# Padding the slots of the split weight tiles by 64 bytes in a two-block fp32 network

## The chip, the cores and the metric

One core of a Trainium2 chip runs the whole program. The metric is device time in microseconds, the median of three runs. The kernel before takes 2099.29 us (2099.01 to 2099.45).

## The reference

Two blocks of a sequence model act on x (512 positions, 1024 features, fp32). Cut to what matters:

```python
# first block
proj = rms_norm(x) @ w_in                        # 1024 -> 7184
merged = g_ml*(mlstm(...) @ w_br_ml) + g_na*(neighbourhood(...) @ w_br_na) + g_xa*(cross(...) @ w_br_xa)
x = x + merged @ w_out
x = x + (gelu(conv3(a)) * u) @ w_down            # a, u = split(rms_norm(x) @ w_up), 1024 -> 2 x 2816 -> 1024
# second block, layer 0
x = x + (b * conv3(c * h)) @ w_out               # b, c, h = split(rms_norm(x) @ w_in)
x = x + (silu(conv3(a)) * g) @ w_down            # the same feed-forward shape
# second block, layer 1
x = x + gated_forgetting_attention(x) @ w_out    # 16 heads of 64
x = x + (silu(conv3(a)) * g) @ w_down
out = rms_norm(x)
```

Nearly all of the arithmetic is products of a 512 x 1024 (or 512 x 2816) activation with an fp32 weight matrix.

## The kernel before

Activations are kept transposed: features on the 128 partitions, the 512 positions along the free axis, so a 1024-feature activation is `KB` = 8 blocks of 128 x 512. A weight matrix is cut into **units** of 128 output features. A unit is one 128 x 1024 tile, whose 8 blocks of 128 x 128 are the stationary operands; the activation block is the moving operand.

To be accurate enough each fp32 value is held as two values of the type fp32r, a high and a low part. Activations have XH and XL (for the feed-forward FH and FL, for others AH/AL, YH/YL, GH/GL). Weights have WH and WL. Each block of a unit takes three matmuls (`unit`, lines 1652 to 1654, and the same triple in other functions): high weights on high activations, high weights on low activations, low weights on high activations.

```python
mm(dst[:, 0:width], WH[:, s, w], a, ...)   # w = slice(k * P, (k + 1) * P)
mm(dst[:, 0:width], WH[:, s, w], b, ...)
mm(dst[:, 0:width], WL[:, s, w], a, ...)
```

A unit passes through four steps, each on its own engine, over `NSLOT` = 4 slots of the tiles RAW, WH and WL:

- SP issues the load of the raw unit into `RAW[:, s, :]`.
- ACT rounds it to WH (`hi`, line 655, one instruction of 1024 columns).
- POOL writes RAW minus WH to WL (`lo`, line 519, four instructions of 256 columns).
- PE multiplies.

The slot is the unit's number modulo four. The loops are unrolled by multiples of four, so each slot's address is a constant of the instruction.

A few places use the slots differently. `forget_unit` (lines 1949 and 1950) takes 48 columns of each block. `lo_gate` and `lo_forget` see a slot as blocks of 32 or 128 columns with a rearranged view. `value_blocks` (lines 1965 to 1967) exchanges the roles: there blocks of XH and XL are stationary, and 512 columns of WH or WL are moving. The attention parts are plain fp32, not fp32r, and don't use these tiles. In `bout_ends` copies of the last blocks stand in tiles of their own.

Where tiles lie is written by hand. `fixed` places them one after another, and X begins at a multiple of 512 bytes (`line`). In each partition X, XH, XL, RAW, WH and WL then take 16 KiB each, the small tiles follow, and after them, at the next multiple of 512, the `zone` that the later tiles share (function `at`, offsets in KiB). A block of 128 weights is 512 bytes of a partition, so every stationary block in WH and WL begins at a multiple of 512 bytes, and so does every moving block of 512 columns.

Of the kernel before, what the change touches and what calls it, by code (L numbers as in the profile page):

```python
# [13 lines left out]
F32R = mybir.dt.float32r  # L14
ALU = mybir.AluOpType
ACT = mybir.ActivationFunctionType
AX = mybir.AxisListType

P = 128
# [8 lines left out]
NSLOT = 4  # L28
LO_PARTS = 4
UW = KB * P  # L30
EPS = 1e-6
NEG = -1e30
ML_H, XA_H, FA_PAIRS, NA_PAIRS = 4, 4, 8, 4
# [155 lines left out]
def two_blocks(nc, A, out):  # L189
# [4 lines left out]
    def fixed(name, shape, dt=F32):  # L194
        t = nc.alloc_sbuf_tensor_at(name, shape, dt, offset=top[0])
        n = 4
        for d in shape[1:]:
            n *= d
        top[0] += (n + 31) // 32 * 32
        return t  # L200
# [13 lines left out]
    XH = fixed("XH", [P, KB, S], F32R)  # L214
    XL = fixed("XL", [P, KB, S], F32R)
    RAW = fixed("RAW", [P, NSLOT, UW])
    WH = fixed("WH", [P, NSLOT, UW], F32R)
    WL = fixed("WL", [P, NSLOT, UW], F32R)
    R = fixed("R", [P, S])
    RM = fixed("RM", [P, M])  # L220
    SS = fixed("SS", [P, S])
# [17 lines left out]
    PAR = fixed("PAR", [P, NCOL])  # L239
    UT = fixed("UT", [P, TB, 64])  # L240
    zone = (top[0] + line - 1) // line * line
    assert zone + 91 * 1024 <= nc.sbuf_usable_end, (zone, nc.sbuf_usable_end)

    def at(name, kib, shape, dt=F32):
        n = 4
        for d in shape[1:]:
            n *= d
        assert kib * 1024 + n <= 91 * 1024
        return nc.alloc_sbuf_tensor_at(name, shape, dt, offset=zone + int(kib * 1024))

    Y = at("Y", 0, [P, 12, S])
    MEMT = at("MEMT", 0, [P, KB, M])
    SX = at("SX", 24, [P, 2, S])
    PT = at("PT", 28, [P, 2, S])
    PB = at("PB", 32, [P, 2, S])
# [59 lines left out]
    hi_ready, lo_ready, unit_done = sem("hi_ready"), sem("lo_ready"), sem("unit_done")  # L315
# [67 lines left out]
    def width(u):  # L383

        j = u - U["merge"]
        return UW // 2 if 0 <= j < len(MRG) and MRG[j][0] == "br" else UW

# [4 lines left out]
    def f_name(p, s):  # L392

        return ("k", "q")[s] if p < FA_LAST else ("q", "k")[s]
# [5 lines left out]
    def f_bank(p, use):  # L400

        return LB[(O["fa"] + FA_L * p + FA_USE[p][use]) % 2]
# [13 lines left out]
    def _(sp):  # L416
        def load(u0, j, i, per, src, width):

            s = (u0 + j) % NSLOT
            if u0 + j >= NSLOT:  # L420
                sp.wait_ge(lo_ready, i * per + (u0 + j - NSLOT + 1))
            sp.dma_start(RAW[:, s, 0:width], src).then_inc(raw_full[s], 16)

        def stream(name, w, iters, per):

            with sp.Fori(0, iters) as i:
                for j in range(per):
                    load(U[name], j, i, per, w[bass.ds(i * per + j, 1), :, :].rearrange("o p n -> p (o n)"), UW)

# [12 lines left out]
        for u in range(NATT):  # L442
            load(0, u, 0, 0, A["w_att"][u, :, :], UW)
            if u < 2:
# [67 lines left out]
    def _(pool):  # L512
        def lo(u0, j, i, per):
# [3 lines left out]
            for c in range(parts):  # L517
                w = slice(c * UW // LO_PARTS, (c + 1) * UW // LO_PARTS)
                last = nc.gpsimd.tensor_tensor(WL[:, s, w], RAW[:, s, w], WH[:, s, w].bitcast(F32), ALU.subtract)  # L519
                if u0 == 0 and j < 2 and c < parts - 1:  # L520
# [3 lines left out]
        def lo_forget():  # L524

            s = U["f"] % NSLOT
            pool.wait_ge(hi_ready, U["f"] + 1)
            raw, w = (t[:, s, :].rearrange("p (k c) -> p k c", c=P) for t in (RAW, WH))
            nc.gpsimd.tensor_tensor(w[:, :, 32:48], raw[:, :, 0:16], w[:, :, 0:16].bitcast(F32), ALU.subtract)\
                .then_inc(lo_ready, 1)  # L530

        def lo_gate(u):

            s = u % NSLOT
            pool.wait_ge(hi_ready, u + 1)
            raw, w = (t[:, s, :].rearrange("p (n c) -> p n c", c=32) for t in (RAW, WH))
            pool.wait_ge(r_ready, 1)
            nc.gpsimd.memset(SS[:], 0.0)
            pool.drain()
            nc.gpsimd.tensor_tensor(w[:, :, 16:32], raw[:, :, 0:16], w[:, :, 0:16].bitcast(F32), ALU.subtract)\  # L540
                .then_inc(lo_ready, 1)
# [5 lines left out]

        for t, v in ((TA[:, 0:P], 1.0), (TA[:, P:2 * P], 0.0), (IDN[:], 0.0), (LO[:], 1.0), (UP[:], 1.0), (EPSC[:], EPS), (ZERO[:], 0.0)):
            nc.gpsimd.memset(t, v).then_inc(consts, 1)
        pool.wait_ge(consts, 7)  # L550
        nc.gpsimd.tensor_copy(ONER[:], TA[:, 0:P])
        nc.gpsimd.memset(EPSC[:, 1:2], EPS * EPS)
        nc.gpsimd.memset(TA[0:64, P:P + 64], 1.0)
# [11 lines left out]
        for u in range(NATT):  # L565
# [4 lines left out]
            if u in BIAS_UNITS:  # L570

                p, v = BIAS_UNITS[u]
# [25 lines left out]
        los("up1", 11, 4)  # L598
        los("down1", 2, 12)
        lo_forget()  # L600

        def causal(dst, src):
# [20 lines left out]
        def lo_parted(n):  # L623
# [3 lines left out]
            for w in [slice(c * 2 * P, min((c + 1) * 2 * P, KEND)) for c in range(LO_PARTS)]:  # L627
                nc.gpsimd.tensor_tensor(WL[:, s, w], RAW[:, s, w], WH[:, s, w].bitcast(F32), ALU.subtract)
            nc.gpsimd.tensor_tensor(WEL[:, n, :], RAW[:, s, KEND:UW], WEH[:, n, :].bitcast(F32), ALU.subtract)\
# [14 lines left out]
    def _(act):  # L644
        A_ = nc.scalar.activation

        def hi(u0, j, i, per):

            if not isinstance(i, int) or u0 + j + i * per < NUNITS:
# [4 lines left out]
                w = slice(0, width(u0 + j))  # L654
                A_(WH[:, s, w], RAW[:, s, w], ACT.Copy).then_inc(hi_ready, 1)  # L655

# [53 lines left out]
        for t, (un, st) in enumerate(SLOTS):  # L710
# [21 lines left out]
            if m < 4 * ML_H:  # L732

                h, s = m // 4, m % 4
# [8 lines left out]
                for d in range(2):  # L743
                    w = slice(P * s, S) if d == 0 else slice(0, P * (s + 1))
                    A_(SXM[m % 2][:, d, w], UE[:, h, d, w], ACT.Relu, bias=UT[:, s, 32 * d + h:32 * d + h + 1])
                act.drain()
                for d in range(2):
                    w = slice(P * s, S) if d == 0 else slice(0, P * (s + 1))
# [40 lines left out]
            if un and un[0] in HALF:  # L789
                k = sum(1 for x in UNITS[:u] if x[0] in HALF)  # L790
# [3 lines left out]
                elif un[0] == "mg":  # L794
                    q = un[1]
                    c = (2 - q % 3) * KB + q // 3
# [4 lines left out]
            if t and EXTRA[t - 1][:1] and EXTRA[t - 1][0][:2] == ("tr", "nav"):  # L801

                p = EXTRA[t - 1][0][2]
# [20 lines left out]
        for j, (kind, n, b) in enumerate(MRG):  # L824
            hi(U["merge"], j + AHEAD, 0, 0)
            if kind == "mg":
                done += 1
                c = (2 - b) * KB + n
# [96 lines left out]
        def hi_parted(n):  # L925
# [4 lines left out]
            if n == 0:  # L930
                act.wait_ge(fc_out, 16)
            A_(WH[:, s, 0:KEND], RAW[:, s, 0:KEND], ACT.Copy)
            A_(WEH[:, n, :], RAW[:, s, KEND:UW], ACT.Copy).then_inc(hi_ready, 1)

        def hi_behind(n):

            s = (U["bout"] + n) % NSLOT
            act.wait_ge(raw_full[s], 16 * ((U["bout"] + n) // NSLOT + 1))
            act.wait_ge(bout_read, n - NSLOT + 1)
            A_(WH[:, s, :], RAW[:, s, :], ACT.Copy).then_inc(hi_ready, 1)  # L940

        def squared(p, s):

# [103 lines left out]
        turned(FA_LAST, 0)  # L1047
        exps(FA_LAST, 1)
        hi_behind(4)
        turned(FA_LAST, 1)  # L1050
        exps(FA_LAST, 2)
        hi_behind(5)
        turned(FA_LAST, 2)
        hi_behind(6)
        hi_behind(7)
        residual("bout", 2, 4, 4, "fg2", unrolled=lambda j: None, have=KB - AHEAD)
# [5 lines left out]
    def _(dve):  # L1062
# [457 lines left out]
        def head_sums(p, s):  # L1520

            dve.wait_ge(q_rs, 2 * p + s + 1)
            n = f_name(p, s)
            v.scalar_tensor_tensor(out=SS[:], in0=f_bank(p, n + "s")[:], scalar=64 * EPS, in1=TD[:],
                                   op0=ALU.add, op1=ALU.mult).then_inc(lin_free, 1)
# [108 lines left out]
    def _(pe):  # L1634
        mm = nc.tensor.matmul

        def unit(u0, j, i, per, kc, xh, xl, k0, dst, start=True, stop=True, width=S, ready=None, halfway=None):
# [4 lines left out]
            for k in range(kc):  # L1642
# [10 lines left out]
                mm(dst[:, 0:width], WH[:, s, w], b, start=False, stop=False)  # L1653
                last = mm(dst[:, 0:width], WL[:, s, w], a, start=False, stop=stop and k == kc - 1)  # L1654
            last.then_inc(unit_done, 1)
# [118 lines left out]
        for t, (un, st) in enumerate(SLOTS):  # L1774
# [37 lines left out]
            if un:  # L1812
# [5 lines left out]
                if t == 0:  # L1818
                    for n, (tt, part, ks) in enumerate(START_ORDER):
# [3 lines left out]
                        for k in ks:  # L1823
# [8 lines left out]
                            else:  # L1832
                                if tt < 2 and k < KB - 2:
                                    pe.wait_ge(first_lo[tt], k // 2 + 1)
                                else:
                                    pe.wait_ge(lo_ready, tt + 1)
                                last = mm(bb[:], WL[:, tt, w], XH[:, k, :], start=False, stop=ends)
                        if n == START_LAST[tt]:
# [5 lines left out]
                elif t < 5:  # L1844
# [7 lines left out]
                    for k in range(KB):  # L1852
                        last = mm(b[:], WL[:, t % NSLOT, k * P:(k + 1) * P], XH[:, k, :], start=False, stop=k == KB - 1)
                    last.then_inc(unit_done, 1)
# [20 lines left out]
        def linear(name, iters, per, xh, xl, ready, norm_of=None, halfway=None, two=0):  # L1875


            def part(j, k0, k1):
# [6 lines left out]
                for k in range(k0, k1):  # L1885
# [4 lines left out]
                    mm(bank_[:], WH[:, s, w], b, start=False, stop=False)  # L1890
                    last = mm(bank_[:], WL[:, s, w], a, start=False, stop=k == KB - 1)  # L1891
                if k1 == KB:
# [326 lines left out]
```

## Time and profile before

| what | value |
|---|---|
| median of 3 runs | 2099.29 us |
| profiled execution, first to last instruction (its own time) | 2098.1 us |
| PE busy | 2090.3 us, 9860 matmul records |
| PEld (weight loads) busy | 1709.4 us, 9860 loads |
| POOL busy | 1164.5 us |
| DVE busy | 972.7 us |
| ACT busy | 884.3 us |
| granted TensorE clock, mean | 1.000 |
| DMA | 203.70 MB, 97 GB/s |

The busy time of PE counts records that overlap: a matmul's record begins when its columns begin to stream and ends when the last result has left, so the pace is read from the distance between the starts of two records, not from the duration of one. PEld is the loading of stationary operands, which runs beside PE. Clock 1.000 means that the granted clock was the higher of its two levels, 2.4 GHz, throughout.

### The profile page before, as it was taken

How to read it: one execution, taken by the hardware profiler on the slowest of the kernel's cores; microseconds unless marked ns; L12 is line 12 of the kernel's file. 1: busy time of each engine (PE TensorE's matmuls, PEld its weight loads, DVE VectorE, ACT ScalarE, POOL GpSimd, SP SyncE). 2: the span in 40 equal slices, each digit the busy share in tenths (PEclk: the TensorE clock that was granted, in tenths of full speed). 3: DMA queues.
4: the chain of work that ended last, by engine and by line, in shares of the span. 5: the costliest groups of instructions: out<-in, count | busy, mean ns of one | idle time of the engine just before them, and what ended most of it. 6: DMA issues, size and time to landing. Idle time of an engine off the chain costs nothing.

```text
span 2098.1 us, 29633 instructions
## 1 busy us (share of the span) xinstructions
PE 2090.3 (100%) x9860; PEld 1709.4 (81%) x9860; DVE 972.7 (46%) x1682; ACT 884.3 (42%) x1355; POOL 1164.5 (56%) x1554
## 2 busy tenths in 40 slices
PE   9999999999999999999999999999999999999999
PEld 7788888888888888888888888888777778888887
DVE  6567564334455551234445544213377755545300
ACT  5544556223434343332244344224466655434321
POOL 8553346556555556555455656565544536556653
PEclk9999999999999999999999999999999999999999
DMA  6333222323332333323233333333322213333332
GB/s 234 119 99 114 63 64 70 106 78 123 92 100 93 96 94 102 95 91 100 91 101 100 96 94 89 108 94 101 111 81 81 81 61 101 100 100 90 103 92 76
DMA packets 62667, 203.70 MB, mean 97 GB/s; under 512 B 7056, under 2 KB 8720, under 8 KB 62576
## 3 DMA queue, kind: packets, MB, share of 16 engines
q1 hardware_dynamic: 60624, 201.54, 30.9%
q10 hardware_dynamic: 1952, 0.99, 0.2%
q8 instruction: 52, 0.85, 0.2%
q14 instruction: 39, 0.32, 0.0%
HBM read 199.42 MB, written 2.26 MB: 96 GB/s over the span
## 4 chain that ended last, share of the span: by engine, by line
PE 98%; DVE 1%; DMA 0%; DVEq 0%; ACT 0%; issue 0%; ACTq 0%; SPq 0%
PE bank L1652 28%; PE bank L1654 28%; PE bank L1653 28%; PE bank L1992 1%; PE bank L2018 1%; PE bank L1761 1%; PE bank L2004 1%; PE bank L1706 1%; PE bank L1965 1%; PE bank L1967 1%; PE bank L1966 1%; PE bank L1891 1%; PE bank L1889 1%; PE bank L1890 1%; PE bank L2049 1%; PE bank L1802 1%
## 5 line engine op out<-in xcount | busy, mean ns | idle before, releaser
L519 POOL TENSOR_TENSOR WL<-RAW,WH 128x256 fp32r<-128x256 f32 x1424 | 1105.8, 809 | 865.7 <-ACT WH L655 858.8
L1652 PE MATMUL bank<-XH,WH 128*128 128x512 f32 x1688 | 661.2, 392 | 0.3 <-DVE FG L1571 0.3
L1654 PE MATMUL bank<-XH,WL 128*128 128x512 f32 x1688 | 657.2, 389 | 0.0
L1653 PE MATMUL bank<-XL,WH 128*128 128x512 f32 x1688 | 656.9, 389 | 0.0
L655 ACT ACTIVATE WH<-RAW 128x1024 fp32r<-128x1024 f32 (+1 forms) x366 | 372.9, 1023 | 236.1 <-PE bank L1654 208.4
L1652 PEld LDWEIGHTS bank<-XH,WH 128*128 128x128 f32 x1688 | 316.9, 188 | 68.4 <-issue 2.8
L1654 PEld LDWEIGHTS bank<-XH,WL 128*128 128x128 f32 x1688 | 316.9, 188 | 66.7
L1653 PEld LDWEIGHTS bank<-XL,WH 128*128 128x128 f32 x1688 | 317.0, 188 | 64.5
L1652 PE MATMUL bank<-FH,WH 128*128 128x512 f32 x528 | 205.4, 389 | 0.0
L1653 PE MATMUL bank<-FL,WH 128*128 128x512 f32 x528 | 205.4, 389 | 0.0
L1654 PE MATMUL bank<-FH,WL 128*128 128x512 f32 x528 | 205.4, 389 | 0.0
L1399 DVE TENSOR_TENSOR X<-X,bank 128x512 f32 (+1 forms) x48 | 32.9, 685 | 292.4 <-PE bank L1654 283.9
L882 ACT ACTIVATE TD<-TC 128x512 f32<-128x512 f32 x66 | 41.7, 632 | 278.0 <-DVE TC L1143 188.0
L1143 DVE SCALAR_TENSOR_TENSOR TC<-TA,PAR,TC 128x511 f32<-128x511 f32 (+1 forms) x134 | 108.9, 813 | 22.4 <-issue 21.8
L1653 PEld LDWEIGHTS bank<-FL,WH 128*128 128x128 f32 x528 | 99.1, 188 | 20.7
L1654 PEld LDWEIGHTS bank<-FH,WL 128*128 128x128 f32 x528 | 99.1, 188 | 20.7
L1652 PEld LDWEIGHTS bank<-FH,WH 128*128 128x128 f32 x528 | 99.1, 188 | 20.4
L1429 DVE TENSOR_TENSOR TA<-bank,R 128x512 f32<-128x512 f32 x66 | 45.6, 691 | 124.1 <-PE bank L1654 116.1
L1434 DVE TENSOR_TENSOR TE<-bank,R 128x512 f32<-128x512 f32 x66 | 45.6, 691 | 110.0 <-PE bank L1654 110.0
L885 ACT ACTIVATE FH<-TA 128x512 f32 x66 | 41.8, 633 | 126.3 <-DVE TA L1438 126.3
L1440 DVE TENSOR_TENSOR FL<-TA,FH 128x512 f32 x66 | 60.1, 911 | 61.7 <-ACT FH L885 61.7
L849 ACT ACTIVATE XH<-X,PAR (+1 forms) x40 | 29.0, 724 | 134.9 <-DVE X L1399 134.9
(336 smaller groups left out, 2618.5 us busy)
## 6 DMA issues: line engine op xcount, KB each, us to landing
RAW<-in_w_up SPq DMA_DIRECT2D x132, 512.0 KB, 3.5
RAW<-in_w_att SPq DMA_DIRECT2D x50, 512.0 KB, 3.6
RAW<-in_w_down SPq DMA_DIRECT2D x48, 448.0 KB, 3.2
RAW<-in_w_down SPq DMA_DIRECT2D x24, 512.0 KB, 3.5
RAW<-in_w_ain SPq DMA_DIRECT2D x24, 512.0 KB, 3.4
RAW<-in_w_fa SPq DMA_DIRECT2D x24, 512.0 KB, 3.6
RAW<-in_w_mrg SPq DMA_DIRECT2D x15, 512.0 KB, 3.9
RAW<-in_w_mrg SPq DMA_DIRECT2D x24, 256.0 KB, 2.7
```

The costliest lines, as they stand in the source:

```text
L519: last = nc.gpsimd.tensor_tensor(WL[:, s, w], RAW[:, s, w], WH[:, s, w].bitcast(F32), ALU.subtract)
L655: A_(WH[:, s, w], RAW[:, s, w], ACT.Copy).then_inc(hi_ready, 1)
L882: A_(TD[:], TC[:], fn).then_inc(glu_ready, 1)
L885: A_(blk(FH, i * 2 + n), TA[:], ACT.Copy).then_inc(ffh_ready, 1)
L1143: last = v.scalar_tensor_tensor(out=TC[:, -d:S], in0=c[:, 0:S + d], scalar=w[k], in1=TC[:, -d:S], op0=ALU.mult, op1=ALU.add)
L1399: v.tensor_tensor(blk(X, nn), blk(X, nn), b[:], ALU.add).then_inc(lin_free, 1)
L1429: v.tensor_tensor(TA[:], LB[0 if (O[name] % 2) == 0 else 1][:], R[:], ALU.mult)\
L1434: v.tensor_tensor(TE[:], LB[1 if (O[name] % 2) == 0 else 0][:], R[:], ALU.mult)\
L1440: v.tensor_tensor(blk(FL, nn), TA[:], blk(FH, nn).bitcast(F32), ALU.subtract).then_inc(ffl_ready, 1)
L1652: mm(dst[:, 0:width], WH[:, s, w], a, start=start and k == 0, stop=False)
L1653: mm(dst[:, 0:width], WH[:, s, w], b, start=False, stop=False)
L1654: last = mm(dst[:, 0:width], WL[:, s, w], a, start=False, stop=stop and k == kc - 1)
```

## The change

A slot of WH and of WL becomes 1040 values long instead of 1024; the last 16 values (64 bytes) are never written or read. RAW keeps 1024. The places that took a whole slot of WH now name its first 1024 columns.

Worked out from the code: WH still begins at a multiple of 512 bytes, and its slots s = 0 to 3 now begin at the remainders 0, 64, 128 and 192 of 512. WH is 256 bytes longer, so WL begins at the remainder 256, and its slots at 256, 320, 384 and 448. WL is 256 bytes longer too, so all that follows it moves by 512 bytes, and so does the zone: their remainders stay as they were. Only the bound on the zone's size falls, from 91 to 90 KiB. The order and the number of instructions on all engines, and of the DMAs, are the same.

```diff
+WPAD = 16
...
-    WH = fixed("WH", [P, NSLOT, UW], F32R)
-    WL = fixed("WL", [P, NSLOT, UW], F32R)
+    WH = fixed("WH", [P, NSLOT, UW + WPAD], F32R)
+    WL = fixed("WL", [P, NSLOT, UW + WPAD], F32R)
...
-    assert zone + 91 * 1024 <= nc.sbuf_usable_end, (zone, nc.sbuf_usable_end)
+    assert zone + 90 * 1024 <= nc.sbuf_usable_end, (zone, nc.sbuf_usable_end)
...
-        assert kib * 1024 + n <= 91 * 1024
+        assert kib * 1024 + n <= 90 * 1024
...
@@ lo_forget
-            raw, w = (t[:, s, :].rearrange("p (k c) -> p k c", c=P) for t in (RAW, WH))
+            raw, w = (t[:, s, 0:UW].rearrange("p (k c) -> p k c", c=P) for t in (RAW, WH))
...
@@ lo_gate
-            raw, w = (t[:, s, :].rearrange("p (n c) -> p n c", c=32) for t in (RAW, WH))
+            raw, w = (t[:, s, 0:UW].rearrange("p (n c) -> p n c", c=32) for t in (RAW, WH))
...
@@ the rounding of a unit of the attention's output product, on ACT
-            A_(WH[:, s, :], RAW[:, s, :], ACT.Copy).then_inc(hi_ready, 1)
+            A_(WH[:, s, 0:UW], RAW[:, s, :], ACT.Copy).then_inc(hi_ready, 1)
```

## Rows read from the trace of the kernel before

**Rows 1.** The page: span, then busy time and instructions by engine.

```profile
span 2098.1 us, 29633 instructions
...
PE 2090.3 (100%) x9860; PEld 1709.4 (81%) x9860; DVE 972.7 (46%) x1682; ACT 884.3 (42%) x1355; POOL 1164.5 (56%) x1554
```

**Rows 2.** The page, chain that ended last: shares of the span by line.

```profile
PE bank L1652 28%; PE bank L1654 28%; PE bank L1653 28%; PE bank L1992 1%; PE bank L2018 1%; PE bank L1761 1%; PE bank L2004 1%; PE bank L1706 1%; PE bank L1965 1%; PE bank L1967 1%; PE bank L1966 1%; PE bank L1891 1%; PE bank L1889 1%; PE bank L1890 1%; PE bank L2049 1%; PE bank L1802 1%
```

**Rows 3.** Whole span, L1652 alone: PE busy (x), PEld busy (x), PEclk, DMA share, GB/s.

```profile
0.00:2098.10 2098.10, 1012.11 (x2600) 488.29 (x2600) 1.00 0.31 97
```

**Rows 4.** Timeline of PE from 599.8 us: start us, us, line, operands, shape.

```profile
599.81 0.39 PE L1652 MATMUL bank<-XH,WH 128*128 128x512 f32 x1
600.04 0.39 PE L1653 MATMUL bank<-XL,WH 128*128 128x512 f32 x1
...
603.89 0.39 PE L1652 MATMUL bank<-XH,WH 128*128 128x512 f32 x1
```

**Rows 5.** Timeline of PE's weight loads (PEld) at 600 us.

```profile
599.81 0.19 PEld L1653 LDWEIGHTS bank<-XL,WH 128*128 128x128 f32 x1
```

**Rows 6.** Timeline of PE, forget unit: stationary operands of 48 columns from WH.

```profile
1440.38 0.40 PE L1949 MATMUL bank<-XH,WH 128*48 128x512 f32 x1
...
1444.15 0.39 PE L1965 MATMUL bank<-WH,XH 128*128 128x512 f32 x1
```

**Rows 7.** Weight loads of three lines: duration ns min/median/max, first and last start.

```profile
L1652 PEld LDWEIGHTS bank<-XH,WH x1688: 186/188/192, 38.4 to 1974.1; 128*128 128x128 f32 x188
...
L1950 PEld LDWEIGHTS bank<-XL,WH x8: 122/122/124, 1440.4 to 1443.7; 128*48 128x48 f32 x8
...
L2018 PEld LDWEIGHTS bank<-FP,FY x320: 132/137/138, 1524.8 to 1709.2; 128*64 128x64 f32 x160
```

**Rows 8.** Timeline of PE, memory keys: moving operands of 256 columns.

```profile
85.28 0.28 PE L1653 MATMUL bank<-ML,WH 128*128 128x256 f32 x1
...
86.00 0.28 PE L1653 MATMUL bank<-ML,WH 128*128 128x256 f32 x1
```

**Rows 9.** Timeline of PE, mLSTM heads in plain fp32: products, scores.

```profile
223.72 1.05 PE L1761 MATMUL bank<-V,PT 128*128 128x129 f32 x8
224.61 0.39 PE L1761 MATMUL bank<-V,PB 128*128 128x129 f32 x2
...
230.32 1.02 PE L1802 MATMUL bank<-Q,K 128*128 128x512 f32 x2
231.18 0.38 PE L1761 MATMUL bank<-V,PT 128*128 128x129 f32 x2
...
330.14 0.61 PE L1761 MATMUL bank<-V,PT 128*128 128x129 f32 x4
330.58 0.61 PE L1761 MATMUL bank<-V,PB 128*128 128x129 f32 x4
```

**Rows 10.** Timeline of PE, after a wait at 508 us.

```profile
507.99 0.50 PE L1652 MATMUL bank<-GH,WH 128*128 128x512 f32 x1 [0.22 <-DVE X L1399]
508.33 0.40 PE L1653 MATMUL bank<-GL,WH 128*128 128x512 f32 x1
...
510.66 0.39 PE L1654 MATMUL bank<-GH,WL 128*128 128x512 f32 x1
```

**Rows 11.** First 50 us, all engines' busy time (x); then PEclk, DMA share, GB/s.

```profile
2.00:50.00 48.00, 47.06 (x220) 37.02 (x219) 30.22 (x59) 28.96 (x50) 40.65 (x72) 1.00 0.69 249
```

**Rows 12.** Timeline of PE at 16 us.

```profile
16.12 1.07 PE L1831 MATMUL bank<-XL,WH 128*128 128x512 f32 x4
17.03 1.07 PE L1837 MATMUL bank<-XH,WL 128*128 128x512 f32 x4
```

**Rows 13.** Groups by line, ACT and POOL, that fill WH and WL.

```profile
L655 ACT ACTIVATE WH<-RAW 128x1024 fp32r<-128x1024 f32 x342 | 358.2, 1051 | 231.5 <-PE bank L1654 203.8 <-PE bank L1967 12.9 <-PE bank L1853 6.6
...
L519 POOL TENSOR_TENSOR WL<-RAW,WH 128x256 fp32r<-128x256 f32 x1424 | 1105.8, 809 | 865.7 <-ACT WH L655 858.8 <-ACT WH L940 3.6 <-DMA CB<-forget_scratch 1.8
...
L628 POOL TENSOR_TENSOR WL<-RAW,WH 128x256 fp32r<-128x256 f32 x12 | 11.7, 1004 | 18.7 <-ACT WEH L933 18.7
```

## Prediction

> **What bounds the kernel now.** I read the page's busy times first, then the chain, then PE's own timeline. PE is busy 2090.3 of 2098.1 us, and the next engine, POOL, 1164.5 [rows 1]. The chain goes through PE's lines 1652, 1653 and 1654 for 28% of the span each, all of them fp32r matmuls with a block of WH or WL as stationary operand [rows 2]. L1652 runs 2600 times, the other two of its triple as often, and the granted clock is 1.00, the 2.4 GHz level, over the whole span [rows 3]. So the time is a number of matmuls times their pace, and a change that moves no instruction can act only through the pace, or by making another engine late.
>
> The pace is read from starts. From 599.81 to 603.89 us lie 18 matmuls: 4.08 / 18 = 0.2267 us each [rows 4]. At 2.4 GHz 512 columns take 213.3 ns, so each matmul pays 13.3 ns over its columns. That excess is what this change can touch. The load of the next stationary block starts together with the current matmul [rows 4, 5] and takes 188 ns [rows 7], so both operands are read at once, and before the change both begin at the remainder 0 of 512 bytes. The trace holds no fp32r matmul with another pair of remainders; this has to be bounded.
>
> **The change, part by part.**
>
> *Instructions, DMAs, queues.* None is added, removed or moved; RAW, the target of the weight loads from HBM, keeps its addresses. Cost 0.
>
> *The writers of WH and WL.* They write to starts that are multiples of 64 bytes. ACT takes 1.051 us for a unit and POOL 4 x 0.809 = 3.24 us [rows 13], while PE takes 24 x 0.2267 = 5.44 us. These 2.2 us are the cover. The slowest row with POOL's same operation is 1.004 us [rows 13], which would make 4.02 us, still below 5.44. POOL's ops would have to grow by two thirds to be late. I take 0 for both ends.
>
> *Moving operands from WH and WL* occur in lines 1965 to 1967, 192 matmuls. The nearest row is the plain fp32 product with V as moving operand, whose blocks begin 516 bytes apart. At V's first block, remainder 0, eight records take 0.89 us, 111 ns each; at a block with remainder 24 four take 0.44 us, 110 ns each [rows 9]. Even a start off the 16 bytes costs a moving operand nothing there. I take 0; if each of the 192 paid the 1 ns that this reading can hide, it would be 0.2 us.
>
> *The stationary reads.* By the counts, 3 x 2600 = 7800 matmuls [rows 3], and about 520 more of the same form in the smaller functions, read WH or WL as stationary operand: 8320. Only slot 0 of WH stays at remainder 0, and it serves two matmuls in three of every fourth unit, one sixth. So 6930 matmuls get new starts. What do they pay or save each?
>
> - For the load by itself the nearest row is line 2018: its 64-column blocks begin in turn at the remainders 0 and 256, and all 320 loads take 132 to 138 ns [rows 7]. A different remainder doesn't lengthen a load there.
> - Does the excess come from the amount of weights that is read beside the stream? Blocks of 48 columns load in 122 ns instead of 188 [rows 7], yet their 16 matmuls take (1444.15 - 1440.38) / 16 = 235.6 ns [rows 6], more and not less. With 256 moving columns the pace is 0.72 / 6 = 120 ns, that is 106.7 + 13.3: the same excess for half the stream [rows 8]. An excess that doesn't shrink with the load and doesn't grow with the stream looks like a hand-over between blocks, not like collisions of two reads.
> - Does other traffic matter? At 16 us, where the DMAs are at 0.69 of their time and POOL is busy 40.65 of 48 us [rows 11], four matmuls take 0.91 us, 227 ns each [rows 12], as at 600 us. Reads and writes by others at many addresses don't stir PE's pace.
>
> So I take 0 for this too. The bounds: the fastest full pace in the trace without the excess is that of plain fp32, where two records of 2 x 512 columns take 0.86 us, 430 ns each or 215 ns for 512 columns [rows 9]; 227 - 215 = 12 ns less on 6930 matmuls is -83 us. On the other side stands the pace of the 48-column blocks, 235.6 ns: +9 ns x 6930 = +62 us.
>
> Here a page speaks against the change. The Trainium skill ("TensorE: Matmul & The Clock Gate", Part 2) says that PE has two independent read ports and that loading the next weights takes nothing from the running matmul; it gives 215.7 ns as the distance of two such matmuls. By the first statement the sum is 0 whatever the addresses; by the figure, an estimate, 11 ns x 6930 = 76 us would be to gain if addresses were what separates this kernel from it. The trace agrees with the first in that traffic leaves the pace alone, and disagrees with the figure by 11 ns.
>
> Sum: 0 + 0 + 0 + 0. The profiled execution spans 2098.1 us [rows 1]; the median of the runs, 2099.29, is 1.2 us more, which lies outside the first and last instruction and stays. Forecast 2099.3 us. A measurement of this kernel tells 0.2%, 4.2 us, from no change.
>
> **The rivals.**
>
> *The beat is lost (slower).* PE's pace is not rigid. After a wait at 507.99 us ten matmuls of the same form take 2.33 us, 233 ns each, and only then does the pace settle at 227 [rows 10, 4]. The 48-column blocks never settle [rows 6]. So the 227 ns are a state into which load and stream fall, and I can't show that this state doesn't need equal starts. If shifted blocks keep the unsettled pace, 6930 x (233 - 227 = 6 ns) = +42 us: 2141; at the 48-column pace +62: 2161. It decides where the pace in the long stretches is over 228 ns, since 0.6 ns x 6930 is 4.2 us. For it: these rows, and that seven of eight slots would be in the new state. Against: the settled pace is the same with XH, FH, AHL, YH and GH as moving operand.
>
> *A crossing costs a little (slower).* A block of 512 bytes that starts at 64 now reaches over a multiple of 512. If each crossing costs one cycle of 2.4 GHz, 0.42 ns, it is 2.9 us, inside the noise; at four cycles 11.5 us: 2111. The loads at remainder 256 [rows 7] are against it only weakly, since their 256 bytes end before the next multiple. By the Trainium skill ("SBUF — State Buffer", Specifications) the line of this memory is 16 bytes; a block at any multiple of 64 still fills 32 whole lines, and by that no crossing is added, so the sum by it is 0. No run here shows that figure.
>
> *The excess is a collision of equal starts (faster).* If load and stream begin together in the same piece of the memory and get in each other's way, shifted starts remove it: 6930 x 12 ns = 83 us, 2016; if half of the shifted pairs still collide, 2058. For it: both start together [rows 4, 5], and plain fp32, which streams its moving columns twice for each load, has no such excess [rows 9]. Against: the 48 columns [rows 6], and a slot's WH and XH differ from block to block by every multiple of 512 without any difference in pace.
>
> *The change does nothing that it says.* The starts are constants of the instructions, so they do move; this is part of the forecast.
>
> **How the numbers follow.** No change in pace 0.56, and with it 2095 to 2103.5. The lost beat 0.18. A crossing that shows 0.08. The collision 0.18. The sum over signs: faster 0.18, same 0.56, slower 0.26. The range must leave out at most 2 in 10. The collision gives 2016 to 2058, far away, and is left out but for 0.02 for a small part of it; of the lost beat the part above 2150, 0.04, is left out. So 2090 to 2150, with the middle case on its lower side.
>
> **What would show it.** Right: PE's distance of starts in the long stretches is still 0.2267 us with WH and with WL, the loads take 188 ns, and POOL's idle time before line 519 stays near 866 us. The lost beat would show as starts 231 to 236 ns apart in units of all slots but WH's first, without settling. The collision would show as 215 ns in the same places. A crossing would show as 227.1 to 228.4. If instead PE waited for ACT or POOL at line 1652, my cover for the writers would be wrong. The forecast is wrong if the pace of slots 1 to 3 differs from that of slot 0.

## The result and the profile after

The change makes the kernel slower: 2129.63 us (median of 4 runs, 2128.79 to 2129.97) against 2099.37, a ratio of 1.0144 with a 95% interval of 1.013 to 1.0158. That is 30.3 us, in a range that had been given as 2090 to 2150; "no change" was forecast as the likeliest.

The page of the changed kernel: its span, and busy time by engine. The answer to [rows 1].

```profile
span 2127.8 us, 29633 instructions
...
PE 2120.8 (100%) x9860; PEld 1711.9 (80%) x9860; DVE 965.7 (45%) x1682; ACT 884.5 (42%) x1355; POOL 1168.9 (55%) x1554
```

The span grew by 29.7 us and PE's busy time by 30.5; the number of instructions is the same, and DVE, ACT and POOL are busy as long as before within 1%. So PE is still the bound, and it does the same work more slowly. (The profiler models where a matmul's record ends; what follows is read from starts.) Whole span, line 1653 of the changed kernel (1652 of before) with its loads, in the columns of [rows 3]; then the loads of that line by themselves, as in [rows 7].

```profile
0.00:2127.80 2127.80, 1021.35 (x2600) 489.00 (x2600) 1.00 0.31 96
...
L1653 PEld LDWEIGHTS bank<-XH,WH x1688: 186/188/192, 38.4 to 2001.6; 128*128 128x128 f32 x188
```

The clock is at 1.00, the 2.4 GHz level, and a load still takes 188 ns. POOL's group that fills WL, the answer to [rows 13]:

```profile
L520 POOL TENSOR_TENSOR WL<-RAW,WH 128x256 fp32r<-128x256 f32 x1424 | 1110.1, 813 | 890.2 <-ACT WH L656 885.1 <-ACT WH L941 3.7 <-issue 1.3
```

813 ns against 809: the writers don't mind the new starts. POOL's idle time before this line grew by 24.5 us, and PE doesn't wait for it: PE is idle for 7.0 us of the whole span, against 7.8 before.

The loss stands in the timeline. These rows of PE are the first matmuls of five units in a row of the first feed-forward up stage (units 24 to 28 of its 44, in the slots 0, 1, 2, 3 and 0).

```profile
673.57 0.39 PE L1653 MATMUL bank<-XH,WH 128*128 128x512 f32 x1
...
679.02 0.40 PE L1653 MATMUL bank<-XH,WH 128*128 128x512 f32 x1
...
684.62 0.39 PE L1653 MATMUL bank<-XH,WH 128*128 128x512 f32 x1
...
690.20 0.39 PE L1653 MATMUL bank<-XH,WH 128*128 128x512 f32 x1
...
695.71 0.39 PE L1653 MATMUL bank<-XH,WH 128*128 128x512 f32 x1
```

A unit has 24 matmuls, so their starts tell the pace of each slot. The units take 5.45, 5.60, 5.58 and 5.51 us: 227, 233, 232 and 230 ns. Before, every unit takes 5.44 us, 24 x 226.7 ns [rows 4]. **The pace has become a property of the slot.** Slot 0, with WH at the remainder 0 and WL at 256, pays nearly nothing; slot 1 (64 and 320) pays most.

Over the units 9 to 44 of the three feed-forward up stages the mean distance of starts is 227.1, 233.2, 232.3 and 229.6 ns, 230.6 over all. If all 8320 matmuls of the form paid these 3.9 ns more, it would be 32 us: the whole loss and a little more.

### The profile page after: what moved, and what is told of

It reads as the page before. It is cut to its first block, busy times and chain, and to the rows that moved or that the text cites. A ratio compares the mean times of both kernels' runs of the same rounds, so it can differ in the third digit from the quotient of the medians.

```text
span 2127.8 us, 29633 instructions
## 1 busy us (share of the span) xinstructions
PE 2120.8 (100%) x9860; PEld 1711.9 (80%) x9860; DVE 965.7 (45%) x1682; ACT 884.5 (42%) x1355; POOL 1168.9 (55%) x1554
## 4 chain that ended last, share of the span: by engine, by line
PE 99%; DVE 1%; DMA 0%; ACT 0%; DVEq 0%; issue 0%; SPq 0%; ACTq 0%
PE bank L1653 28%; PE bank L1655 28%; PE bank L1654 28%; PE bank L1993 1%; PE bank L2019 1%; PE bank L1762 1%; PE bank L2005 1%; PE bank L1707 1%; PE bank L2050 1%; PE bank L1966 1%; PE bank L1968 1%; PE bank L1967 1%; PE bank L1891 1%; PE bank L1890 1%; PE bank L1892 1%; PE bank L2052 1%
```

## The experiments

All runs are compared with the kernel before on the same chip, 2099.3 to 2099.7 us there. Each kernel here ran once, at a granted clock of 1.00; the runs of the kernel before lie within 0.7 us of each other. A **distance** below is the start of a stationary block minus the start of the moving operand, in bytes, modulo 256. The paces are means over the last half of a unit, units 9 to 44 of the three up stages, so that the first matmuls after a change of slot, where the pace still settles, don't count.

Three theories stood at the start. Theory 1: the distance between stationary and moving operand sets the pace. Theory 2: the start of the stationary block by itself does. Theory 3: different remainders among neighbouring blocks do.

The diffs show the lines that matter, against the changed kernel. `begin(rem)` puts the next tile at the remainder `rem` of 512 bytes, and with `WPAD = 0` the slots are 1024 values long again.

**The later tiles moved, the slots as before.**

```diff
-WPAD = 16
+WPAD = 0
...
-    top[0] = (top[0] + line - 1) // line * line
+    def begin(rem):
+
+        top[0] = (top[0] - rem + line - 1) // line * line + rem
+
+    begin(0)
     X = fixed("X", [P, KB, S])
...
+    begin(0)
     RAW = fixed("RAW", [P, NSLOT, UW])
+    begin(0)
     WH = fixed("WH", [P, NSLOT, UW + WPAD], F32R)
+    begin(0)
     WL = fixed("WL", [P, NSLOT, UW + WPAD], F32R)
+    begin(0)
+    top[0] += 512
...
-    zone = (top[0] + line - 1) // line * line
+    begin(0)
+    zone = top[0]
```

> Slots as before, but 512 unused bytes behind WL, so that all later tiles lie 512 bytes higher, as in the change. All three theories expect 2099 us and a pace of 226.7 ns in every slot; anything above 2104 would say that the place of the later tiles, not the remainders, made the loss.

Measured: 2099.42 us, 226.7 ns in every slot. First matmuls of the units 24 and 25 of the first up stage, 5.44 us apart:

```profile
665.98 0.39 PE L1663 MATMUL bank<-XH,WH 128*128 128x512 f32 x1
...
671.42 0.39 PE L1663 MATMUL bank<-XH,WH 128*128 128x512 f32 x1
```

The shift of the later tiles by 512 bytes costs nothing.

**All weights at 64, moving operands at 0.** As the edit above, but:

```diff
+    begin(64)
     WH = fixed("WH", [P, NSLOT, UW + WPAD], F32R)
+    begin(64)
     WL = fixed("WL", [P, NSLOT, UW + WPAD], F32R)
+    begin(0)
+    top[0] += 0
```

> No padding; WH and WL both begin at remainder 64, moving operands at 0. Theory 1 (the distance of the remainders of stationary and moving operand sets the pace): slot 1 of the change has this distance and runs at 233.3 ns, so 8324 x 6.6 ns = +55 us, about 2154 us, 233 ns in every slot. Theory 2 (the stationary block's own start counts, it has to be at a multiple of 256): the same 2154 us. Theory 3 (what hurts is that WH and WL, or neighbouring slots, have different remainders): 2099 us.

Measured: 2149.40 us, 5 us under the 2154 of theory 1. The same two units of this kernel, first matmuls, are 5.60 us apart, 233.3 ns a matmul, and so it is in all four slots:

```profile
678.84 0.39 PE L1663 MATMUL bank<-XH,WH 128*128 128x512 f32 x1
...
684.44 0.39 PE L1663 MATMUL bank<-XH,WH 128*128 128x512 f32 x1
```

Theory 3 falls: all weights have the same remainder here, and the loss is larger than that of the change.

**Both at 64.**

```diff
+    begin(64)
     X = fixed("X", [P, KB, S])
...
+    begin(0)
     RAW = fixed("RAW", [P, NSLOT, UW])
+    begin(64)
     WH = fixed("WH", [P, NSLOT, UW + WPAD], F32R)
+    begin(64)
     WL = fixed("WL", [P, NSLOT, UW + WPAD], F32R)
+    begin(64)
+    top[0] += 0
...
+    begin(64)
+    zone = top[0]
```

RAW stays at a multiple of 512.

> Both begin at remainder 64: X, XH, XL, the small tiles and the zone, and WH and WL too. Theory 1 (distance): distance 0 again, 2099 us, 226.7 ns. Theory 2 (own start of the stationary block): about 2154 us, 233 ns. Theory 3 (different remainders among neighbours): 2099 us.

Measured: 2099.29 us. The same two units are 5.44 us apart again:

```profile
665.87 0.39 PE L1663 MATMUL bank<-XH,WH 128*128 128x512 f32 x1
...
671.31 0.39 PE L1663 MATMUL bank<-XH,WH 128*128 128x512 f32 x1
```

Theory 2 falls: every stationary block begins at 64 and reaches over a multiple of 512, as in the run before, and nothing is lost. The moving operands begin at 64 too, so their own start by itself costs nothing either. ACT and POOL write to the same remainders in both runs, so it isn't the writers either.

**Only the moving operands at 64.** As the edit above, with `begin(0)` ahead of WH and of WL.

> WH and WL begin at remainder 0 as before, the moving operands and the zone at 64. Theory 1 (distance): the distance is 192 of 256, as in slot 3 of the change, which settles at 228.9 ns: 8324 x 2.2 ns = +18 us, about 2117 us. Theory 2 (own start of the stationary block): 2099 us. Theory 3 (different remainders among neighbours): 2099 us. If instead a moving operand off the multiple of 512 costs by itself, anything above 2099 in this run and in the one that shifts both.

Measured: 2123.93 us, with the weights where they lay before. First matmuls of three units of the first up stage, then of three of the last:

```profile
670.02 0.39 PE L1663 MATMUL bank<-XH,WH 128*128 128x512 f32 x1
...
675.51 0.39 PE L1663 MATMUL bank<-XH,WH 128*128 128x512 f32 x1
...
681.00 0.39 PE L1663 MATMUL bank<-XH,WH 128*128 128x512 f32 x1
...
1872.38 0.40 PE L1663 MATMUL bank<-XH,WH 128*128 128x512 f32 x1
...
1877.98 0.40 PE L1663 MATMUL bank<-XH,WH 128*128 128x512 f32 x1
...
1883.58 0.40 PE L1663 MATMUL bank<-XH,WH 128*128 128x512 f32 x1
```

In the first two up stages every unit takes 5.49 to 5.50 us, 228.9 ns a matmul, the pace of slot 3 of the change, as theory 1 has it. In the last up stage every unit takes 5.60 us, 233.3 ns, at the same distance. The down stage behind it is at 233.3 ns too, the two before at 228.9. So sign and mechanism are theory 1's, and its number, 2117 us, is 7 us short because one distance can hold two paces: the last up and down stage have about 1580 of these matmuls, and 4.4 ns more on each make these 7 us. What decides between them I take to be the state in which a stage is entered; that isn't shown, since no run varies it by itself. (128 does the same: 231.7 ns in slot 2 of the change, 233.3 in the map below.)

These four runs show the cause: **the pace hangs on how the starts of PE's two operands lie to each other, not on either by itself, and equal starts are a good place.** That it is the distance is borne out by 192: it gave 228.9 ns by shifted weights, in slot 3 of the change, and by shifted moving operands, in two stages of three. Whether equal starts are the best place was open.

**A map in steps of 16 bytes.** Four kernels, each with four slots at four distances (WH and WL of a slot alike).

`WOFF` is 4, 20, 36 and 52 values, so the first slot begins at 16, 80, 144 and 208 bytes; the edit of the last:

```diff
-WPAD = 16
+WPAD = 4
+WOFF = 52
...
-    WH = fixed("WH", [P, NSLOT, UW + WPAD], F32R)
-    WL = fixed("WL", [P, NSLOT, UW + WPAD], F32R)
+
+    def slots(name):
+
+        top[0] = (top[0] + line - 1) // line * line
+        n = NSLOT * (UW + WPAD)
+        t = fixed(name, [P, (WOFF + n + 7) // 8 * 8], F32R)
+        return t[:, WOFF:WOFF + n].rearrange("p (s n) -> p s n", s=NSLOT)
+
+    WH, WL = slots("WH"), slots("WL")
+    top[0] = (top[0] + line - 1) // line * line
```

> Slots 0 to 3 of both tiles begin at distances 16, 32, 48 and 64 from the moving operands (WH and WL of a slot at the same distance). Both theories: slot 3 at 233.3 ns as in the run with all weights at 64. Theory 1a (equal starts are the best place; every other distance costs): slots 0 to 2 between 227 and 234 ns, the run at 2115 to 2155 us. Theory 1b (0 is only a good place; the excess of 13 ns over the columns is itself a collision that another distance avoids): one of the slots below 226 ns, down to 215 ns.

> Distances 80, 96, 112 and 128. Both theories: slot 3 at 231.7 to 232.4 ns, as slot 2 of the change. Theory 1a: all slots 228 to 234 ns, the run at 2110 to 2155 us. Theory 1b: one of them may lie below 226 ns.

> Distances 144, 160, 176 and 192. Both theories: slot 3 at 229 to 230.4 ns, as slot 3 of the change and the run with moved moving operands. Theory 1a: all slots 228 to 234 ns, the run at 2110 to 2150 us. Theory 1b: one of them may lie below 226 ns.

> Distances 208, 224, 240 and 256. If the pattern repeats every 256 bytes, slot 3 is at 226.7 ns as distance 0; if it repeats only every 512, at anything else. Theory 1a: slots 0 to 2 between 227 and 231 ns, the run at 2105 to 2125 us. Theory 1b: one of them below 226 ns; just below the equal start is the likeliest place, since the load begins a few ns after the stream.

Measured: 2149.07, 2149.43, 2137.58 and 2126.81 us. The paces in ns:

| distance | 16 | 32 | 48 | 64 | 80 | 96 | 112 | 128 |
|---|---|---|---|---|---|---|---|---|
| pace | 233.3 | 233.3 | 233.3 | 233.3 | 232.0 | 234.2 | 233.3 | 233.3 |

| distance | 144 | 160 | 176 | 192 | 208 | 224 | 240 | 256 |
|---|---|---|---|---|---|---|---|---|
| pace | 233.3 | 233.3 | 230.0 | 228.9 | 232.2 | 233.3 | 228.3 | 226.7 |

First matmuls of the five units in the last of these kernels, distances 208, 224, 240, 256 and 208:

```profile
673.02 0.40 PE L1662 MATMUL bank<-XH,WH 128*128 128x512 f32 x1
...
678.59 0.39 PE L1662 MATMUL bank<-XH,WH 128*128 128x512 f32 x1
...
684.19 0.40 PE L1662 MATMUL bank<-XH,WH 128*128 128x512 f32 x1
...
689.69 0.40 PE L1662 MATMUL bank<-XH,WH 128*128 128x512 f32 x1
...
695.15 0.40 PE L1662 MATMUL bank<-XH,WH 128*128 128x512 f32 x1
```

The units at 224 and 256 take 5.60 and 5.46 us. Distance 256 settles at the pace of 0 (after four matmuls that do not keep it yet), so the pattern repeats every 256 bytes, as far as this distance and WL at 256 in slot 0 of the change can show. No slot is below 226 ns: 1b falls, and theory 1a stands in what it says of the sign. Some of its sizes missed: 208 and 224 (232.2 and 233.3 ns) had been expected at 227 to 231, their run (2126.81 us) at no more than 2125, and 128 (233.3) at 231.7 to 232.4. With equal starts the second 256 columns take 226.7 - 120 = 106.7 ns [rows 4, 8]; by that rate 512 columns take 213.3. Equal starts pay 13.3 ns over this, and 233.3, the value that comes most often, 20.

**Steps of 4 bytes around the equal start.** The same edit with `WPAD = 1`, and `WOFF = 0` or 61.

> Distances 0, 4, 8 and 12 bytes. Slot 0 settles at 226.7 ns. If the load and the stream meet in lines of 16 bytes, slots 1 to 3 behave nearly as slot 0, 226.7 to 229 ns; if any distance off 0 breaks the settled state, 231 to 234 ns as at 16. A slot below 226 ns would be a version to build. POOL and ACT may take longer on starts that are no multiple of 16, but have 2.2 us of cover in a unit.

> Distances 244, 248, 252 and 256, that is 12, 8, 4 and 0 bytes below the equal start. Slot 3 settles at 226.7 ns. Between 228.3 ns (distance 240) and 226.7 for the others if the pace rises step by step; 231 to 234 ns if any distance off 0 breaks the settled state; below 226 ns if the 3 ns by which the load begins after the stream are what costs, since a start a few bytes lower would then meet the stream better.

Measured: 2127.79 and 2117.45 us. Paces in ns:

| distance | 0 | 4 | 8 | 12 | 244 | 248 | 252 | 256 |
|---|---|---|---|---|---|---|---|---|
| pace | 226.7 | 232.4 | 230.8 | 230.0 | 226.7 | 233.3 | 226.7 | 226.7 |

First matmuls of the five units, distances 0, 4, 8, 12 and 0:

```profile
673.44 0.40 PE L1662 MATMUL bank<-XH,WH 128*128 128x512 f32 x1
...
678.91 0.40 PE L1662 MATMUL bank<-XH,WH 128*128 128x512 f32 x1
...
684.49 0.39 PE L1662 MATMUL bank<-XH,WH 128*128 128x512 f32 x1
...
690.03 0.39 PE L1662 MATMUL bank<-XH,WH 128*128 128x512 f32 x1
...
695.54 0.40 PE L1662 MATMUL bank<-XH,WH 128*128 128x512 f32 x1
```

The same in the other kernel, distances 244, 248, 252, 256 and 244:

```profile
671.68 0.39 PE L1662 MATMUL bank<-XH,WH 128*128 128x512 f32 x1
...
677.13 0.39 PE L1662 MATMUL bank<-XH,WH 128*128 128x512 f32 x1
...
682.73 0.39 PE L1662 MATMUL bank<-XH,WH 128*128 128x512 f32 x1
...
688.17 0.40 PE L1662 MATMUL bank<-XH,WH 128*128 128x512 f32 x1
...
693.63 0.39 PE L1662 MATMUL bank<-XH,WH 128*128 128x512 f32 x1
```

244 and 252 settle like 0, with units of 5.45 and 5.44 us, against theory 1a's "every other distance costs"; 248 between them doesn't, with 5.60. One value of four bytes decides, so lines of 16 bytes don't describe it, and neither does a pace that rises step by step; 8 and 12 lie in neither of the two bands that were expected. No settled pace is below 226.7. So none of the 21 unequal distances, each in the one order of slots that ran, beats the equal start, and no version came out that beats the kernel before. POOL, which was thought to take longer at such starts, takes less, 753 ns a piece in the first of these kernels against 809:

```profile
L529 POOL TENSOR_TENSOR WL<-RAW,WH 128x256 fp32r<-128x256 f32 x1424 | 1025.8, 753 | 971.6 <-ACT WH L665 966.0
```

**Which load meets which stream?** XL and WL at 64, WH, XH and all else at 0.

```diff
+    begin(64)
     XL = fixed("XL", [P, KB, S], F32R)
+    begin(0)
     RAW = fixed("RAW", [P, NSLOT, UW])
+    begin(0)
     WH = fixed("WH", [P, NSLOT, UW + WPAD], F32R)
+    begin(64)
     WL = fixed("WL", [P, NSLOT, UW + WPAD], F32R)
+    begin(0)
+    top[0] += 0
```

> Only XL and WL begin at remainder 64; WH, XH and all else at 0. The matmuls of a block are WH on XH, WH on XL, WL on XH. Theory P (a load meets the stream that runs while it loads): WL is loaded while XL streams, both at 64, and WH while XH streams, both at 0, so in the up stages every distance is 0: 226.7 ns; where FH and FL (or AH, YH, GH) move, one load in three has distance 64, between 226.7 and 233.3 ns, in 868 triples at most 868 x 3 x 6.6 ns = 17 us; the run between 2099 and 2117 us. Theory O (a block counts against the operand that it is multiplied with): in the up stages the distances are 0, -64 and 64, a pace of 228 to 233 ns there as well; the run between 2107 and 2150 us.

Measured: 2135.80 us, and 231.9 ns in the up stages. The units 24 and 25 of the first up stage begin 5.57 us apart:

```profile
675.40 0.40 PE L1664 MATMUL bank<-XH,WH 128*128 128x512 f32 x1
...
680.97 0.40 PE L1664 MATMUL bank<-XH,WH 128*128 128x512 f32 x1
```

Theory P, which says that a load meets the stream running beside it in the records, asked for 226.7 ns there: it falls as I put it. Theory O's bounds, 228 to 233 ns and 2107 to 2150 us, hold. PE's timeline in the first down stage, where FH and FL lie at 0 and only WL is shifted:

```profile
850.21 0.39 PE L1665 MATMUL bank<-FL,WH 128*128 128x512 f32 x1
850.44 0.40 PE L1666 MATMUL bank<-FH,WL 128*128 128x512 f32 x1
850.67 0.39 PE L1664 MATMUL bank<-FH,WH 128*128 128x512 f32 x1
850.90 0.39 PE L1665 MATMUL bank<-FL,WH 128*128 128x512 f32 x1
851.13 0.40 PE L1666 MATMUL bank<-FH,WL 128*128 128x512 f32 x1
851.37 0.39 PE L1664 MATMUL bank<-FH,WH 128*128 128x512 f32 x1
```

By means over the three down stages the matmul with WH on FH takes 228.4 ns, the one with WH on FL 229.1, and the one with WL on FH 235.8. The slow one is the one whose own stationary block is shifted, although WH is being loaded beside it. But such a split doesn't tell which matmul is to blame. In the run with only the moving operands at 64, where all three have the same distance, they take 229.2, 231.7 and 225.8 ns in the first down stage, and in the last up stage of the run here the one with WL is the fastest of the three, at 229.2. So theory O, that a block counts against the operand it is multiplied with, is left standing but not shown, and no run has equal starts by O and different ones by P.

## Why the prediction was wrong in its likeliest case

- *PE bounds the kernel, and the change can act only through the pace* was right: PE's busy time took all of the loss.
- *The writers cost 0* was right: 813 ns a piece for POOL, and the run with both sides at 64 has the same writes and no loss.
- *Later tiles, DMAs and queues cost 0* was right, by the run with the shifted tiles.
- *The stationary reads cost 0* is the step that failed; it measured +30 us. Its three reasons didn't bear on the question. The loads of line 2018 begin at remainders 0 and 256, which I took for two places; the map shows that for the pace they are the same place. And a load's own duration isn't where the loss shows: it is 188 ns after the change as before. The 48-column blocks, slower with less to load, were read as "a hand-over, not a collision"; they said that the pace isn't simply columns plus the amount of a load, and nothing about addresses. (An excess that doesn't grow with the stream holds for equal starts only; at distance 64 it is 7 ns for 256 columns and 20 for 512, see the last section.) And that DMAs and POOL don't stir the pace tells nothing of PE's two operands against each other.
- The page of the Trainium skill that I weighed ("TensorE: Matmul & The Clock Gate", Part 2) says that loading the next weights takes no read bandwidth from the running matmul. The runs don't bear out that the two sides can be laid out independently: shifting the moving side alone by 64 bytes costs 24 us, the stationary side alone 50, shifting both nothing.
- *The collision of equal starts* (faster, 0.18) had the sign wrong: equal starts are the good place.
- *The lost beat* (slower, 0.18) is what happened. Its condition was that the settled state needs equal starts, and at the distances of the change that is what the runs show (244 and 252 reach it too). Its price was 6 ns on 6930 matmuls, 42 us; the measured 30.3 us are 4.4 ns on each of these. Mis-sized was the pace that replaces the settled one: I gave the unsettled 233 ns to all shifted slots. Slot 1 has it (233.2), slot 2 nearly so (232.3), slot 3 settles in a better rhythm (229.6), and slot 0 loses next to nothing, since WL's remainder of 256 is as good as 0; so three units in four are slowed, 6240 matmuls and not 6930. (The 228 ns that I gave as the mark of this case is too high: 0.6 ns over 226.7 is 227.3.) The rows of [rows 10], where after a wait ten matmuls stay at 233 ns before 227 is reached, were the right hint. They showed that 227 is a state that has to be reached, and deserved more than 0.18; that its condition is equal starts, they couldn't show.
- *A crossing costs a little* was wrong: with both sides at 64 every block crosses a multiple of 512 for nothing.

## What to carry to other kernels

When a stream of fp32r matmuls with 512 columns and a new stationary block each is the bound, place both operands so that they begin at the same remainder of 256 bytes; shifting one of them alone can cost over 2% (50 us of 2099 here). Other types weren't tried, and shorter streams can want another distance, as the next section shows. A row of the profile that varies something else than the change does, here the size of a load or the traffic of other engines, is no bound for the change; and a pace that is reached only after some matmuls is a state that a change can break.

## What the runs showed of the hardware that I had not expected

A distance of a single 4-byte value changes the pace of fp32r matmuls by 6 ns, 2.5%, and not in order: 244 and 252 are as good as 0, 248 is as bad as 64. Away from equal starts the paces often repeat in a fixed rhythm, and one distance can hold several. At distance 12 starts are 224 and 236 ns apart in turn. At 64 they are 236 and 231 ns apart in turn in slot 1 of the change and in the second up stage of the run with all weights at 64, and even, 233 ns, in its first and last.

And the good distance depends on the moving operand's length. With 256 columns, before, six matmuls take 0.72 us, 120 ns each [rows 8]. In the run with all weights at 64 the memory keys show, with the time of ten matmuls between these two starts,

```profile
85.23 0.28 PE L1665 MATMUL bank<-MH,WL 128*128 128x256 f32 x1
...
86.36 0.28 PE L1663 MATMUL bank<-MH,WH 128*128 128x256 f32 x1
```

1.13 us, 113 ns each: there the unequal start is the faster one. Seven of the eight units of this kind settle at 113 ns in that run, one at 118; with both operands at 64 all settle at 120 as before. Over the 106.7 ns of 256 columns that is an excess of 7 ns against 13. In this kernel these are 192 matmuls, about 1 us. What in the chip makes the rhythm stays open; the runs show only on what it depends: the distance of the two starts modulo 256, the length of the moving operand, and something that differs between stages.
